# Router stage of a one-layer hybrid trunk with a mixture of experts: rows turned unscaled, choice one tile behind, last two tiles placed together

## What is computed

```python
x = x + mixed @ w_out[layer]
h = _rms_norm(x, norm_ffn[layer])
x = x + _hierarchical_moe(h, ...)

g_logits = (xt @ rg_w) + rg_b                     # 4 groups
g_sel = argmax(g_logits); p_group = softmax(g_logits)[g_sel]
e_logits = ((xt @ re_w) + re_b)[group g_sel]      # 8 of 32 experts
top_v, top_i = top_k(e_logits, 2)
gate = p_group * softmax(top_v)
# every (token, choice) is sorted by expert into blocks of 128 rows;
# y = (silu(xb @ w_gate[e]) * (xb @ w_up[e])) @ w_down[e], added back with its gate
```

## Time and profile before

| | |
|---|---|
| median of 3 runs | 1451.56 us (1447.0 to 1452.16) |
| the profiled execution's own time | 1454.74 us |
| its span, first to last instruction | 1452.9 us, 15254 instructions |
| TensorE busy | 1336.4 us, 92% |
| VectorE busy | 506.4 us, 35% |
| ScalarE, GpSimd busy | 251.5 us, 175.2 us |
| mean granted TensorE clock | 0.956 of full speed |

### The profile page before, as it was taken

How to read it: one execution, slowest core, us unless ns; L and a number is a source line. 1 busy time by engine, 2 the same in 40 slices (tenths; PEclk the granted TensorE clock), 3 DMA queues, 4 the chain that set the end, 5 groups by cost and what they waited for, 6 DMA issues and landing times.

```text
span 1452.9 us, 15254 instructions
## 1 busy us (share of the span) xinstructions
PE 1336.4 (92%) x5616; PEld 691.3 (48%) x5616; DVE 506.4 (35%) x1193; ACT 251.5 (17%) x487; POOL 175.2 (12%) x170
## 2 busy tenths in 40 slices
PE   6999999999999888879998679999999999999985
PEld 3444554644446566654555534443444444444432
DVE  2079683133546565651344512111111111111100
ACT  5000114132124333331111010000000000000000
POOL 1000005222000000000000011211212112112111
PEclk9999999899999899999999589999999999999998
DMA  6011010100120110302221098959999999999970
GB/s 256 0 60 58 1 58 0 58 6 6 48 66 5 36 35 5 121 1 93 101 87 73 28 395 338 400 195 350 424 404 406 412 407 391 402 397 389 403 272 18
DMA packets 51272, 261.70 MB, mean 180 GB/s; under 512 B 21571, under 2 KB 21843, under 8 KB 38908
## 3 DMA queue, kind: packets, MB, share of 16 engines
q1 hardware_dynamic: 42684, 243.72, 41.9%
q0 software_dynamic: 8320, 16.81, 4.7%
q10 hardware_dynamic: 192, 0.17, 0.1%
HBM read 247.52 MB, written 23.64 MB: 187 GB/s over the span
## 4 chain that ended last, share of the span: by engine, by line
PE 69%; issue 8%; DMA 7%; DVE 7%; POOL 3%; DVEq 3%; ACT 1%; SPq 0%; POOLq 0%; ACTq 0%
PE ps L1176 18%; PE ps L1178 13%; PE ps L895 9%; PE ps L1081 8%; PE ps L899 4%; DMA arena<-in_ex_up 3%; PE ps L1026 3%; DMA arena<-in_ex_down 2%; PE ps L1057 2%; POOL arena L2020 2%; PE ps L1042 2%; PE ps L1162 1%; PE ps L1102 1%; DMA arena<-in_ex_gate 1%; DVE arena L1495 1%
## 5 line engine op out<-in xcount | busy, mean ns | idle before, releaser
L1176 PE MATMUL ps<-arena 128*128 128x512 f32 x768 | 336.7, 595 | 1.9 <-ACT arena L1971 0.8
L1176 PEld LDWEIGHTS ps<-arena 128*128 128x128 f32 x768 | 144.3, 191 | 171.9 <-issue 169.3
L1178 PE MATMUL ps<-arena 128*64 128x512 f32 x480 | 213.5, 601 | 8.3 <-DMA arena<-in_ex_up 4.5
L1179 PE MATMUL ps<-arena 128*64 128x512 f32 x480 | 213.6, 601 | 0.0
L899 PE MATMUL ps<-arena 128*128 128x512 f32 x384 | 173.6, 605 | 0.0
L895 PE MATMUL ps<-arena 128*128 128x512 f32 x320 | 137.6, 592 | 0.0
L1740 DVE TENSOR_TENSOR arena<-arena,ps 128x512 f32<-128x512 f32 x26 | 17.9, 689 | 328.8 <-PE ps L1176 202.3
L1178 PEld LDWEIGHTS ps<-arena 128*64 128x64 f32 x480 | 64.7, 138 | 138.1 <-issue 136.2
L1081 PE MATMUL ps<-arena 128*128 128x512 f32 x256 | 112.1, 597 | 0.8 <-DVE arena L1532 0.8
L899 PEld LDWEIGHTS ps<-arena 128*128 128x128 f32 x384 | 72.6, 195 | 83.0 <-issue 81.5
L2076 POOL DMA_INDIRECT out<-arena x26 | 42.0, 1615 | 473.2 <-DVE arena L1746 473.2
(11 more groups left out here) (299 smaller groups left out, 1297.7 us busy)
## 6 DMA issues: line engine op xcount, KB each, us to landing
arena<-in_ex_gate SPq DMA_DIRECT2D x32, 2048.0 KB, 21.7
arena<-in_ex_up SPq DMA_DIRECT2D x32, 2048.0 KB, 24.2
arena<-in_ex_down SPq DMA_DIRECT2D x32, 2048.0 KB, 24.0
arena<-in_w_in SPq DMA_DIRECT2D x5, 2048.0 KB, 7.8
arena<-in_x SPq DMA_DIRECT2D x16, 512.0 KB, 6.2
arena<-bias_by_distance SPq DMA_DIRECT2D x4, 1024.0 KB, 5.9
arena<-in_w_out SPq DMA_DIRECT2D x8, 512.0 KB, 7.3
out<-arena SPq DMA_DIRECT2D x8, 512.0 KB, 2.6
```

The source lines that it names most:

```text
L1176: last = mm(ps[:, to, :], rowsT[:, k, :], weights[left][:, k, cols], **f)
L1178: mm(ps[0:HALF, to, :], rowsT[:, k, 0:HALF], weights[left][:, k, cols], **f)
L1179: last = mm(ps[HALF:P, to, :], rowsT[:, k, HALF:P], weights[right][:, k, cols], **f)
```

## The change

- **Turning.** TensorE turns the residual rows `xs` themselves (`turn_x2`), between the two halves of the next tile's output product. `norm_ffn` is multiplied into the router's rows once (VectorE, `router_sb`), and the row's norm `rs` is multiplied in when the logits are read, in the instruction that adds the bias. The router matrix has 40 columns: 4 groups, 4 columns of zero whose bias is -3e38, 32 experts, so that the copy to a padded row goes. The scaled rows are still made and stored for the gather.
- **Order.** Logits, choice and ranks come one tile sooner: logits of t-1 after the second half of tile t, with the list of t-2; ranks of t-2 after the turn in mid-product. Waits follow (`rank_sb`: the ranks were read).
- **Choice.** Three copies or casts are gone, the index is compared as it is.
- **Placing.** `place` works on n tiles at once, and tiles 6 and 7 are placed together after the last choice. Two subtractions of 1 are folded into constants. The expert numbers are cast after the first of the last four operand pairs.
- **Other engines.** SP's load of x waits for the turn too. ScalarE's two exponentials come after the copies of the lists. The 2048 columns of `hg` are cleared by GpSimd.

```diff
             def out_rows(t, half):
-                if t >= 2:
+                if t >= 2 and half == 0:
                     pe.wait_ge(x2_done, t - 1)
...
+            def turn_x2(t):
+                pe.wait_ge(x2_done, t + 1)
                 if t:
                     pe.wait_ge(h2T_done, t)
                 for k in range(KC):
+                    last = tr(ps[:, 4 + k // 4, (k % 4) * P:(k % 4 + 1) * P], xs[:, t % 2, k * P:(k + 1) * P], ident)
                 last.then_inc(h2_turned, 1)
             def logits_of(t):
                 pe.wait_ge(h2T_done, t + 1)
                 if t == 0:
+                    pe.wait_ge(router_sb, 1)
+                else:
                     pe.wait_ge(logit_sb, t)
+                if t:
+                    pe.wait_ge(rank_sb, min(t, TILES - 2))
...
-            for t in range(TILES + 4):
-                for stage_of, behind in ((out_rows, 0), (logits_of, 2), (list_of, 4), (ranks_of, 3), (turn_h2, 1)):
-                    if 0 <= t - behind < TILES:
-                        stage_of(t - behind)
-                if t == TILES + 2:
-                    experts_by_rank()
+            for t in range(TILES):
+                out_rows(t, 0)
+                if t:
+                    turn_x2(t - 1)
+                if t >= 2:
+                    ranks_of(t - 2)
+                out_rows(t, 1)
+                if t:
+                    logits_of(t - 1)
+                if t >= 2:
+                    list_of(t - 2)
+            turn_x2(TILES - 1)
+            logits_of(TILES - 1)
+            pe.wait_ge(logit_sb, TILES)
+            ranks_of(TILES - 2)
+            ranks_of(TILES - 1, 96)
+            experts_by_rank()
+            list_of(TILES - 2)
+            list_of(TILES - 1)
             rows_by_rank()
...
             def choose(t):
                 v.wait_ge(logit_mm, t + 1)
-                tt(logits[:, t, :], ps[:, 6, 0:36], par[:, P_RBIAS:P_RBIAS + 36], ALU.add)
+                v.wait_ge(x2_rs, t + 1)
+                stt(logits[:, t, :], ps[:, 6, 0:8 + EXPERTS], rs[:, t:t + 1], par[:, P_RBIAS:P_RBIAS + 8 + EXPERTS],
+                    ALU.mult, ALU.add)
...
-            def place(t):
+            def place(t0, n):
...
+                for t in range(t0, t0 + n):
+                    for c in range(2):
+                        at_least(v, list_mm, 2 * t + c - 1)
...
                         nc.vector.drain().then_inc(list_v, 1)
+                        if last and (t, c) == (t0, 0):
+                            v.wait_ge(order_mm, 1)
+                            nc.vector.tensor_copy(expert_of[0:1, :], ps[0:1, 4, 0:EXPERTS])
+                            nc.vector.drain().then_inc(experts_known, 1)
...
-            for t in range(TILES + 3):
-                for stage_of, behind in ((residual, 0), (choose, 2), (place, 3), (gained, 0)):
...
+            for t in range(TILES):
+                residual(t)
+                if t:
+                    choose(t - 1)
+                gained(t)
+                if 1 <= t < TILES - 1:
+                    place(t - 1, 1)
+            choose(TILES - 1)
+            place(TILES - 2, 2)
+            tt(gexp, logits[:, :, 0:4], gtop[:, :, 0:1].to_broadcast([P, TILES, 4]), ALU.subtract)
+            tt(e_diff, etop[:, :, 1], etop[:, :, 0], ALU.subtract)
+            nc.vector.drain().then_inc(route_v, 1)
...
+            pool.wait_ge(out_mm, TILES)
+            nc.gpsimd.memset(hg, 0.0).then_inc(hg_zero, 1)
             pool.wait_ge(hg_zero, 1)
```

More of the change, by code:

```diff
@@ L356, in build @@
         g_ffn = cut(B + 2048, D)
-        router = cut(B + 3072, KC, 36)
-        logits = cut(B + 3360, TILES, 36)
+        router = cut(B + 3072, KC, 8 + EXPERTS)
+        logits = cut(B + 3400, TILES, 8 + EXPERTS)
         h2s = cut(H, 2, D)
@@ L382, in build @@
         before = cut(r0 + 1664, TILES, EXPERTS)
-        rtmp = cut(r0 + 2176, 2, EXPERTS)
+        rtmp = cut(r0 + 2176, 2, 2, EXPERTS)
         e_count = cut(r0 + 2432, EXPERTS)
@@ L1074, in _, with out_rows @@
             pe.wait_ge(cv_out, 2)
-            def out_rows(t):
-                if t >= 2:
+            def out_rows(t, half):
+                if t >= 2 and half == 0:
                     pe.wait_ge(x2_done, t - 1)
[L1079 to L1086, removed]
+                for k in range(KC):
+                    last = mm(ps[:, 2 * (t % 2) + half, :], mixT(k, t),
+                              w_out[k][:, half * 512:(half + 1) * 512], start=(k == 0), stop=(k == KC - 1))
+                if half:
+                    last.then_inc(out_mm, 1)
+            def turn_x2(t):
+                pe.wait_ge(x2_done, t + 1)
                 if t:
@@ L1630, in _ @@
-            nc.vector.memset(padded, -3e38)
+                stt(rmod[:, :, ts_], jn[:, :, ts_], -float(P), rk_k[:, :, ts_], ALU.mult, ALU.add)
+                tt(jhot[:, :, ts_, :], over_block(jn[:, :, ts_]), blocks(C_J), ALU.is_equal)
+                done = nc.vector.drain()
+                if last:
+                    done.then_inc(order_done, 1)
+                for c in range(2):
+                    stt(jhot[:, c, ts_, :], cst[:, C_TOK + t0:C_TOK + t0 + n].unsqueeze(2).to_broadcast([P, n, 8]),
+                        float(c * SEQ + 1), jhot[:, c, ts_, :], ALU.add, ALU.mult)
@@ new lines, in place @@
+                nc.vector.drain()
+                for t in range(t0, t0 + n):
+                    for c in range(2):
+                        at_least(v, list_mm, 2 * t + c - 1)
+                        ts(r_hot[:, c, :], cst[:, C_IOTA:C_IOTA + P], rmod[:, c, t:t + 1], -1.0, ALU.subtract, ALU.is_equal)
+                        tt(r_val[:, c, :].rearrange("p (j e) -> p e j", j=8), bc_h(hot[:, c, t, :], 8),
+                           bc_f(jhot[:, c, t, :], EXPERTS), ALU.mult)
+                        nc.vector.drain().then_inc(list_v, 1)
+                        if last and (t, c) == (t0, 0):
+                            v.wait_ge(order_mm, 1)
+                            nc.vector.tensor_copy(expert_of[0:1, :], ps[0:1, 4, 0:EXPERTS])
+                            nc.vector.drain().then_inc(experts_known, 1)
@@ new lines, in _ @@
+            tt(router, router, par[:, P_GFFN:P_GFFN + KC].unsqueeze(2).to_broadcast([P, KC, 8 + EXPERTS]), ALU.mult)
+            nc.vector.drain().then_inc(router_sb, 1)
+            for t in range(TILES):
[8 more added lines that the diff above has]
+            tt(gexp, logits[:, :, 0:4], gtop[:, :, 0:1].to_broadcast([P, TILES, 4]), ALU.subtract)
```

126 lines of the change are left out of this document (45 added, 81 removed).

## The result

The changed kernel takes **1436.81 us** (median of 4 runs, 1432.2 to 1438.92) beside 1451.86 us for the kernel before (4 runs, 1447.0 to 1455.32): ratio **0.9894, interval 0.9857 to 0.9932**, 15 us less. The forecast was 1433.9 in a range of 1428 to 1441, so the measured median lies inside it, 2.9 us above its middle value. Two later series of the same kernel, on two different chips, gave 0.9852 (0.9818 to 0.9885) and 0.9862 (0.983 to 0.9895); the three together, 15.1, 21.2 and 18.7 us, mean 18.3 us less.

The account below looks back on a forecast made before the run. The chain of waits between last output product and first expert product was taken to set the time: placing -19.5, lists +2.1, gather -0.3, so -17.7 us at the expert stage's start, giving 1433.9 us, range 1428 to 1441.

Parts of the forecast that it names:

- The bound: Between last output product and first expert product: a chain of waits; 1 us shorter there makes the kernel about 1 us shorter.
- Rival (d): Expert stage gives the gain back because weights arrive no earlier: 1442 if waits doubled, 1451.6 if all lost; chance 0.02.
- The output stage: Output products with more small groups between and inside them: costs 3.4 us (3.1 to 5.9).
- the 2.4 us that went: Output stage: time beyond products and small groups, nearly all where ranks waited 0.41 us for logits and the clock fell.
- Rival (c): Output stage: the clock falls between product halves, 14 dips of 2.4 us, giving 1467.5 us; chance 0.03.
- The tail to the last placing: From the last output product's end to the last placing's start: 12.5 us (11.6 or 13.3), 19.5 us earlier than before.
- Behind the placing: From the last placing to the gather: cast at 3.45 us, weights requested at 5.0, lists ended at 8.1, gather near 13.
- +2.1 for lists in line: Behind the last placing: four list products one behind the other end at 8.1 us in place of 6.0.
- The gather: First gather in the tail: meets less traffic as weights are requested 8 us before it; 0 to -0.6 us, taken as -0.3.
- GpSimd's fill: Clearing 2048 columns on GpSimd in the tail: 1.9 us long, cost taken as 0, at most +1.9 if VectorE were held.
- Rival (a): TensorE keeps the high clock level in all of the tail: up to 3 us more, about 1428.6 us; chance 0.07.
- Rival (b): A new wait (fill holding VectorE, late x2 loads, longer lists) takes part of the gain: 1439 to 1444 us; chance 0.08.

Follow-up runs that it names:

- the two held gathers: Changed kernel with four or twelve more GpSimd fills before the first gather: 1439.56 and 1455.77 us, tails 39.68 and 54.61 us.
- old_order_new_steps: Changed kernel with the earlier order, scaled rows turned and single placing, keeping shorter steps, early cast and GpSimd's fill: 1447.56 us, ratio 0.9966 to the kernel before.
- turn_scaled: Changed kernel, but TensorE turns the scaled rows and the router is not scaled: 1437.09 us, tail 38.89 us; repeated 1440.03 us, tail 38.03 us.
- place_apart: Changed kernel, but tiles 6 and 7 are placed one after the other, the first list between: 1436.32 us, tail 32.63 us.
- tail_reordered: Changed kernel with tile 7's turned rows copied in halves, tile 5's list after tile 7's logits, tile 7's scaling after its choice: 1433.64 us, tail 30.36 us.
- tail_lean: Changed kernel with the last tile's copy, list and scaling reordered, plus 9 unused matmuls in TensorE's waits of the tail: 1429.53 us, tail 28.34 us.
- changed_again: The changed kernel itself, unaltered, in a second series: 1431.01 us, ratio 0.9852 to the kernel before.
- changed_third: The changed kernel itself, unaltered, in a third series: 1429.45 us, ratio 0.9862 to the kernel before.

## Why the prediction was right, point by point

- **The bound.** That the kernel follows the tail one to one: shown by the two held gathers for a longer tail, and for the change's shorter one by the part behind it, which kept its length. Rival (d), the gain given back in the expert stage, falls for this change: from the first expert product on it is 605.95 to 609.97 us in three profiles, around the 608.09 of before. Its waits for weights rose only from 8.3 to 9.2 us, as this group of the kernel after shows (busy us, mean ns, idle before, releasers):

```profile
L1193 PE MATMUL ps<-arena 128*64 128x512 f32 x480 | 213.5, 601 | 9.2 <-DMA arena<-in_ex_down 4.5 <-DMA arena<-in_ex_up 4.5 <-DMA arena<-in_ex_gate 0.2
```

- **The output stage.** Small groups of 23.5 us and eight products of 109.9 with 0.6 for the rest gave 134.0; it was 133.82. The 0.6 is right in size, 133.82 - 109.9 - 23.5 = 0.4, and so is "0 to 0.1 us a change". But **the reason given for the 2.4 us that went is not shown**, and one run speaks against it. The prediction put the dip in the earlier trace rows down to the wait of ranks for the logits. old_order_new_steps has the same wait of the same length, and no dip behind it (timeline of TensorE):

```profile
721.49 0.38 PE L1113 MATMUL ps<-arena 128*128 128x32 f32 x2 [0.41 <-DVEq L1562]
...
721.93 1.07 PE L1092 MATMUL ps<-arena 128*128 128x128 f32 x8
722.83 13.90 PE L1082 MATMUL ps<-arena 128*128 128x512 f32 x32
```

  So a gap of 0.41 us doesn't bring a dip each time; with the same order the stage lasts 128.87 us there, where it was 130.54. The 1.67 us between them are the dip (0.7 in the turn before the product, 0.96 in the product), and of the 13 profiles other than that of before none has one. The wait itself, 0.41 us, is a second part of the 2.4, and that part did go with the new order, as the prediction said. Whether the dip belongs to the kernel before or to that one execution stays open; the price of the change in this stage is 3.3 us against a stage with the dip and 4.95 against one without.
- **Rival (c), dips between the halves.** None came: seven turns and six rank groups in mid-product, clock 1.00. The rule of the Trainium skill that spoke for it (TensorE: Matmul & The Clock Gate, Part 4, transposes do not count as activity) is not borne out at this spacing: each turn is 1.04 us between half products of 7 us. In the tail, where real idle time stands before a turn (turn_scaled, 3.49 us), the turn itself ran low at 1.96.
- **The tail to the last placing.** Predicted 12.5 between 11.6 and 13.3, by not deciding at which level the last logits run; measured 12.0. The level was the high one in this profile (1.98 us), and their end came at 6.8 us, as in that branch (799.45 - 792.63). The choice of tile 7 took 3.23 us (799.45 to 802.68) where 2.9 was said, and ranks with totals 1.95 (802.68 to 804.63), at the low level as said, where 1.75 was. (The prediction's printed terms add up to 11.45 and 13.15, not 11.6 and 13.3.) In the two further profiles, where those logits took 2.52 and 2.49 us, the placing starts at 12.55 and 12.53, so the middle value was met, by logits at neither level throughout: neither branch was decided, and the closeness is luck.
- **Behind the placing.** Expert numbers cast 3.66 us behind its start (3.45 said), weights requested at 4.9 (5.0), the lists' end at 8.19 (8.1; 808.26 + 4.56 - 804.63), the first gather at 13.3 (13). In the two further profiles, with lists and gather by rank partly at the high level, it comes at 12.3 and 12.4. The +2.1 for lists in line stands; place_apart shows that the other way of placing costs as much.
- **The gather.** It was to take 0.3 us less in less traffic, a size that no row of before gave. The chain in order of time of the kernel after has it at 4.51 us, against 4.59 in the earlier trace rows, so the term is 0.1, and whether traffic is its cause isn't shown:

```profile
817.97 4.51 DMA arena<-h_rows,arena
```

- **GpSimd's fill.** 1.80 us (1.9 said), ended at 797.9, beside the choice of tile 6. VectorE's steps beside it are no longer than alone: the two-input step of L1590 is 0.22 us at 796.93 and 0.23 at 801.83. So the cost is 0, the value taken from a bound of 1.9. The Trainium skill, SBUF — State Buffer, section "SBUF: two separate sides", says the same of an instruction of GpSimd that reads no SBUF; here the trace agrees.
- **Rival (a), high level all through the tail.** It did not come by itself; in the two further profiles it came for parts of the tail. Forced by fillers it brought 2.0 us in the reordered tail (tail_reordered to tail_lean), less than the "up to 3 us" put on it. **Rival (b), a new wait:** the tail has none; its waits are those of the forecast.
- **What the median added.** The sum by stages (-18.03) was nearer to the forecast (-17.7) than the median is: 2.9 us above it, though the profiled time (1437.14) is within 0.2 of the 1437.0 worked out for it. Both agreements hold in part by terms that cancel: to the last placing the stretch from the first output product fell by 20.2 us (19.5 said), and behind it grew by 2.1 (1.8 said). The prediction took 3.2 us off as the distance of the profiled execution from the median of before; in the first series of the changed kernel that distance was 0.3, in the later ones 1.8 and 5.3. That correction is noise of the size of the error.

## What to carry to other kernels

Where a stage is full of TensorE work and followed by a chain of small dependent steps, count in the trace how many rounds of that chain stand behind the last large product: here the rounds that were moved in under the products brought some 12 us of tail, and the unscaled rows some 6 more, for 5 us of stage, while the shorter steps alone brought 3.6. Ask of each producer in the chain whether it needs the value it waits for: multiplying by the norm after the product, not before the turn, took a 3.5 us wait away and with it 2.1 to 2.6 us of low clock behind it (0.9 in the turn, 1.15 to 1.65 in the logits). Look at the lengths of the stages that an edit touches beside the medians, which carry several us of chance from elsewhere: output stage and tail agree to 0.3 us in three profiles of the changed kernel (the tail to 0.9 in two of turn_scaled), while the part behind them differs by 4. A gain that only one stage's length shows, as tail_lean's, is not yet a gain of the kernel.

## What the runs showed of the hardware that was not expected

- **The same instructions end 8.6 us apart.** Up to the output stage all kernels run the same mixers, but the first output product starts between 652.2 and 660.8 us in 14 profiles, in clusters (three at 652.2 to 652.4, one at 655.5, three at 656.7 to 656.8, one at 658.8, six at 660.3 to 660.8). Windows from 560 to 650 us, first before (start 660.26), then turn_scaled (652.40):

```profile
560.00:650.00 90.00, 75.89 (x678) 54.27 (x678) 54.25 (x176) 33.24 (x86) 6.94 (x8) 0.91 0.14 51
```

```profile
560.00:650.00 90.00, 74.45 (x708) 53.77 (x706) 55.89 (x178) 36.73 (x93) 6.93 (x8) 0.96 0.15 51
```

  The first had a clock of 0.91 and 678 matmuls in these 90 us, the second 0.96 and 708 with less busy time. (The windows cut the two at somewhat different points of the same work.) What makes the clock fall in one execution and not in another was not settled; the stretch is one of small products with waits on VectorE and ScalarE between them.
- **The length of a gap does not decide the level.** 0.41 us stood ahead of a dip in one profile and of none in another; behind 1.11 us the last logits took 1.98, 2.52 and 2.49 us in three profiles of the changed kernel itself, as the rows of the two later ones show beside 797.43 above (the first is changed_again, the second changed_third):

```profile
795.38 2.52 PE L1105 MATMUL ps<-arena 128*128 128x40 f32 x16 [1.11 <-ACT arena L1958]
```

```profile
799.46 2.49 PE L1105 MATMUL ps<-arena 128*128 128x40 f32 x16 [1.11 <-ACT arena L1958]
```

- **Fillers grow when they are needed most.** A filler (128x512, two matmul instructions) takes 0.9 us at the high level (3.60 us for four) and 1.8 at the low one (5.42 for three): where the clock has fallen before them, they stood in the way of the work that they were meant to speed up.
- **Clearing 2048 columns** on GpSimd takes 1.80 us, 1.9 times the 0.95 for 1024.
